# A hybrid decoder trunk in float32: four alternating seven-product units per down projection instead of five

## The reference

```python
def swiglu(h, w_gate, w_up, w_down):
    return (jax.nn.silu(h @ w_gate) * (h @ w_up)) @ w_down

x = x + 0.5 * swiglu(rms_norm(x, norm_w[l, 0]), ffn_w_gate[l, 0], ffn_w_up[l, 0], ffn_w_down[l, 0])
x = x + mixer(rms_norm(x, norm_w[l, 1]))
x = x + 0.5 * swiglu(rms_norm(x, norm_w[l, 2]), ffn_w_gate[l, 1], ffn_w_up[l, 1], ffn_w_down[l, 1])
```

## Time and profile before

| | us |
|---|---|
| median of 3 runs | 1131.41 (1130.73 to 1131.84) |
| the profiled execution | 1132.68 |
| its span in the trace | 1130.9 |
| PE busy | 1072.1 (95% of the span) |
| PE weight loads busy | 970.0 (86%) |
| DVE busy | 792.9 (70%) |
| ACT busy | 551.8 (49%) |

### The profile page before, as it was taken

The page is one execution under the profiler, slowest core; times in us unless marked ns, Lnnn a source line. Parts: engine busy times, 40 slices in busy tenths (PEclk is TensorE's granted clock), DMA queues, the critical chain, the costliest instruction groups (busy, mean ns, idle before and its releaser), DMA issues.

```text
span 1130.9 us, 19136 instructions
## 1 busy us (share of the span) xinstructions
PE 1072.1 (95%) x8333; PEld 970.0 (86%) x8333; DVE 792.9 (70%) x1011; ACT 551.8 (49%) x661; POOL 49.2 (4%) x32
## 2 busy tenths in 40 slices
PE   7999988999888999998989999898999999999978
PEld 7999966898777799997779999776788889999957
DVE  5877678698853587676768767676764647667676
ACT  5644345585672354443535444353754536444242
POOL 1000000110171000000000000000100000000000
PEclk9999999999898999999999999999999999999999
DMA  9855436363004275553457565356546465655341
GB/s 312 265 184 188 159 118 203 118 192 112 2 4 152 75 224 186 187 187 107 159 181 224 184 189 187 99 165 220 167 151 218 152 223 167 195 175 196 125 150 38
DMA packets 127197, 184.90 MB, mean 164 GB/s; under 512 B 4205, under 2 KB 101722, under 8 KB 126986
## 3 DMA queue, kind: packets, MB, share of 16 engines
q1 hardware_dynamic: 126368, 181.85, 49.6%
q0 software_dynamic: 448, 1.71, 0.5%
q10 hardware_dynamic: 298, 0.12, 0.0%
HBM read 182.62 MB, written 1.05 MB: 162 GB/s over the span
## 4 chain that ended last, share of the span: by engine, by line
PE 73%; DVE 17%; ACT 5%; issue 3%; DMA 1%; POOLq 0%; SPq 0%; POOL 0%; DVEq 0%; ACTq 0%
PE banks L1441 20%; PE banks L1442 20%; PE banks L1443 20%; DVE wlo L918 8%; ACT whi L482 4%; DVE rounded L996 2%; DVE arena L989 2%; PE banks L1877 2%; DVE raw L991 1%; DVE arena L990 1%; PE banks L1520 1%; PE banks L1524 1%; PE banks L1521 1%; PE banks L1603 1%; PE banks L1604 1%
## 5 line engine op out<-in xcount | busy, mean ns | idle before, releaser
L918 DVE TENSOR_TENSOR wlo<-raw,whi 128x2048 fp32r<-128x2048 f32 (+1 forms) x167 | 381.9, 2298 | 151.2 <-ACT whi L482 150.9
L482 ACT ACTIVATE whi<-raw 128x2048 fp32r<-128x2048 f32 (+1 forms) x171 | 322.9, 1904 | 253.0 <-PE banks L1443 136.5
L1441 PE MATMUL banks<-xTh,whi 128*128 128x256 f32 x1408 | 397.2, 282 | 0.8 <-DVE wlo L918 0.5
L1442 PE MATMUL banks<-xTl,whi 128*128 128x256 f32 x1408 | 396.2, 281 | 0.0
L1443 PE MATMUL banks<-xTh,wlo 128*128 128x256 f32 x1408 | 396.1, 281 | 0.0
L1441 PEld LDWEIGHTS banks<-xTh,whi 128*128 128x128 f32 x1408 | 265.9, 189 | 1.8 <-DVE wlo L918 1.0
L1442 PEld LDWEIGHTS banks<-xTl,whi 128*128 128x128 f32 x1408 | 266.1, 189 | 0.0
L1443 PEld LDWEIGHTS banks<-xTh,wlo 128*128 128x128 f32 x1408 | 266.0, 189 | 0.0
L1441 PE MATMUL banks<-whi,hTh 128*128 128x512 f32 (+1 forms) x180 | 78.5, 436 | 24.4 <-issue 24.3
L1442 PE MATMUL banks<-wlo,hTh 128*128 128x512 f32 (+1 forms) x180 | 74.8, 416 | 0.0
L1443 PE MATMUL banks<-whi,hTl 128*128 128x512 f32 (+1 forms) x180 | 74.5, 414 | 0.0
(11 more groups left out here) (277 smaller groups left out, 1403.1 us busy)
## 6 DMA issues: line engine op xcount, KB each, us to landing
raw<-in_ffn_w_up SPq DMA_DIRECT2D x44, 1024.0 KB, 5.4
raw<-in_ffn_w_down SPq DMA_DIRECT2D x44, 1024.0 KB, 4.9
raw<-in_ffn_w_gate SPq DMA_DIRECT2D x43, 1024.0 KB, 5.4
raw<-in_sg_w_in SPq DMA_DIRECT2D x16, 1024.0 KB, 5.6
raw<-in_ab_w_in SPq DMA_DIRECT2D x8, 1024.0 KB, 5.4
raw<-in_sg_w_out SPq DMA_DIRECT2D x8, 1024.0 KB, 5.3
raw<-in_ab_w_out SPq DMA_DIRECT2D x4, 1024.0 KB, 4.9
raw<-in_ab_w_in SPq DMA_DIRECT2D x2, 832.0 KB, 4.4
```

The source lines that it names most:

```text
L482: A(whi[:, j % SLOTS, 0:kt * width], raw[:, j % SLOTS, 0:kt * width], ACT.Copy).then_inc(S("hi_ready"), 1)
L918: TT(wlo[:, j % SLOTS, 0:n], raw[:, j % SLOTS, 0:n], whi[:, j % SLOTS, 0:n].bitcast(f32), ALU.subtract).then_inc(S("lo_ready"), 1)
L1441: mm(out_ap, lh, rh, start=first, stop=False)
L1442: mm(out_ap, lh, rl, start=False, stop=False)
```

## The change

The seven-product units are 2, 4, 6 and 8, each followed by a direct one. Of such a unit the three plain blocks (1536 columns) are rounded and split apart from the summed block, which goes with T_SUM. The orders on ACT and DVE are written out anew, the third and fourth down units (base + 24, base + 25) are now rounded and split inside the last gate/up pair, and the splits of the next stage's first two units stand among the x_updates. The load behind a seven-product unit waits for the lo of its summed block. The two buffers of T_SUM and T_HI change places.

```diff
-SEVEN = (2, 3, 5, 6, 8)
+SEVEN = (2, 4, 6, 8)
...
-        T_AT = [XT0 + 3072, XT0 + 1536]
-        T_SUM, T_HI, T_LO = [at(o, 1536) for o in T_AT], [at_r(o, 1536) for o in (R0 + 4096, XT0)], [at_r(o, 1536) for o in T_AT]
+        T_AT = [XT0 + 1536, XT0 + 3072]
+        T_SUM, T_HI, T_LO = [at(o, 1536) for o in T_AT], [at_r(o, 1536) for o in (XT0, R0 + 4096)], [at_r(o, 1536) for o in T_AT]
...
         def lo_done(j):
...
-            return S("lo_ready"), j + 1 - sum(1 for i in POOL_LO if i < j)
+            if j in SEVEN_UNITS:
+                n = SEVEN_UNITS.index(j)
+                return S("sums_lo"), 2 * N7 * (n // N7) + N7 + n % N7 + 1
+            return S("lo_ready"), j + 1 - sum(1 for i in POOL_LO + SEVEN_UNITS if i < j)
...
+        SEVEN_UNITS = [u_ffn[f] + 22 + i for f in range(4) for i in SEVEN]
...
             def hi(j):
...
-                A(whi[:, j % SLOTS, 0:kt * width], raw[:, j % SLOTS, 0:kt * width], ACT.Copy
-                  ).then_inc(S("hi_ready"), 1)
+                n = 1536 if j in SEVEN_UNITS else kt * width
+                A(whi[:, j % SLOTS, 0:n], raw[:, j % SLOTS, 0:n], ACT.Copy).then_inc(S("hi_ready"), 1)
...
+            def right_hi(f, k):
+
+                j = u_ffn[f] + 22 + SEVEN[k]
+                act.wait_ge(S("summed"), 2 * N7 * f + N7 + k + 1)
+                A(T_HI[k % 2], T_SUM[k % 2], ACT.Copy).then_inc(S("sums_hi"), 1)
+                A(whi[:, j % SLOTS, 1536:2048], raw[:, j % SLOTS, 1536:2048], ACT.Copy).then_inc(S("sums_hi"), 1)
...
                 for c in range(PAIRS_F):
-                    if c < PAIRS_F - 1:
-                        hi(base + 2 * c + 4)
+                    hi(base + 2 * c + 4)
                     silu_gate(f, c)
-                    if c < PAIRS_F - 1:
-                        hi(base + 2 * c + 5)
+                    hi(base + 2 * c + 5)
                     prod_hi(f, c)
...
+                d = base + 22
+                right_hi(f, 0)
+                hi(d + 4)
+                hi(d + 5)
+                right_hi(f, 1)
+                hi(d + 6)
+                hi(d + 7)
+                right_hi(f, 2)
+                hi(d + 8)
+                hi(d + 9)
+                right_hi(f, 3)
+                hi(d + 10)
+                hi(d + 11)
+                act.wait_ge(S("seven_sums"), 4 * f + 1)
+                A(V1, B[0][:], ACT.Copy).then_inc(S("p1_out"), 1)
+                hi(d + 12)
...
+            def base_lo(j):
+
+                dve.wait_ge(S("hi_ready"), j + 1)
+                TT(wlo[:, j % SLOTS, 0:1536], raw[:, j % SLOTS, 0:1536], whi[:, j % SLOTS, 0:1536].bitcast(f32),
+                   ALU.subtract)
...
             def right_lo(f, k):
...
+                dve.wait_ge(S("sums_hi"), 3 * N7 * f + N7 + 2 * k + 1)
+                TT(T_LO[k % 2], T_SUM[k % 2], T_HI[k % 2].bitcast(f32), ALU.subtract)
+                dve.wait_ge(S("sums_hi"), 3 * N7 * f + N7 + 2 * k + 2)
+                TT(wlo[:, j % SLOTS, 1536:2048], raw[:, j % SLOTS, 1536:2048], whi[:, j % SLOTS, 1536:2048].bitcast(f32),
+                   ALU.subtract).then_inc(S("sums_lo"), 1)
...
-            def next_x(s, factor):
-
-                for q in range(3):
-                    x_update(s - 1, q, factor)
+            def next_x(s, factor, j=None):
+
+                x_update(s - 1, 0, factor)
+                if j is not None:
+                    lo(j)
+                x_update(s - 1, 1, factor)
+                x_update(s - 1, 2, factor)
                 for k in range(4):
                     x_lo(s, k, s)
                 x_update(s - 1, 3, factor)
+                if j is not None:
+                    lo(j + 1)
                 for k in range(4, 8):
                     x_lo(s, k, s)
...
                     if c < PAIRS_F - 1:
                         lo(base + 2 * c + 4)
+                    else:
+                        base_lo(base + 24)
                     scale_up(f, c)
                     product(f, c)
-                    if c < PAIRS_F - 1:
-                        lo(base + 2 * c + 5)
+                    lo(base + 2 * c + 5)
                     prod_lo(f, c)
...
+                d = base + 22
+                right_sums(f, 0)
+                right_lo(f, 0)
+                base_lo(d + 4)
+                right_sums(f, 1)
+                lo(d + 5)
+                right_lo(f, 1)
+                base_lo(d + 6)
+                right_sums(f, 2)
+                lo(d + 7)
+                right_lo(f, 2)
+                base_lo(d + 8)
+                right_sums(f, 3)
+                lo(d + 9)
+                right_lo(f, 3)
+                lo(d + 10)
                 seven_added(f)
-                lo(base + 34)
                 factor = [0.5, 0.5]
                 if f < 3:
-                    next_x(s + 1, factor)
+                    next_x(s + 1, factor, d + 11)
...
                 begin(j)
-                pe.wait_ge(S("sums_lo"), 2 * N7 * f + N7 + k + 1)
                 pe.wait_ge(S("prod_lo"), PAIRS_F * f + i + 1)
```

More of the change, by code:

```diff
@@ L534, in prod_hi, with left_hi @@
                   ).then_inc(S("prod_hi"), 1)
-            def sums_hi(f, k):
+            def left_hi(f, k):
                 act.wait_ge(S("summed"), 2 * N7 * f + k + 1)
                 A(S_HI[k], S_SUM[k], ACT.Copy).then_inc(S("sums_hi"), 1)
+            def right_hi(f, k):
[3 more added lines that the diff above has]
+                A(whi[:, j % SLOTS, 1536:2048], raw[:, j % SLOTS, 1536:2048], ACT.Copy).then_inc(S("sums_hi"), 1)
             def ffn(f):
@@ L552, in ffn @@
                 for c in range(PAIRS_F):
-                    if c < PAIRS_F - 1:
-                        hi(base + 2 * c + 4)
+                    hi(base + 2 * c + 4)
                     silu_gate(f, c)
-                    if c < PAIRS_F - 1:
-                        hi(base + 2 * c + 5)
+                    hi(base + 2 * c + 5)
                     prod_hi(f, c)
                     if c in SEVEN:
[L560 to L571, removed]
+                        left_hi(f, SEVEN.index(c))
+                d = base + 22
[14 more added lines that the diff above has]
+                hi(d + 12)
                 if f < 3:
@@ L976, in left_lo @@
             def left_lo(f, k):
-                dve.wait_ge(S("sums_hi"), 2 * N7 * f + k + 1)
+                dve.wait_ge(S("sums_hi"), 3 * N7 * f + k + 1)
                 TT(S_LO[k], S_SUM[k], S_HI[k].bitcast(f32), ALU.subtract
@@ L993, in right_lo @@
             def right_lo(f, k):
-                dve.wait_ge(S("sums_hi"), 2 * N7 * f + N7 + k + 1)
-                TT(T_LO[k % 2], T_SUM[k % 2], T_HI[k % 2].bitcast(f32), ALU.subtract).then_inc(S("sums_lo"), 1)
+                j = u_ffn[f] + 22 + SEVEN[k]
+                dve.wait_ge(S("sums_hi"), 3 * N7 * f + N7 + 2 * k + 1)
[3 more added lines that the diff above has]
+                   ALU.subtract).then_inc(S("sums_lo"), 1)
             def seven_added(f):
@@ L1080, in ffn @@
                         left_sums(c, SEVEN.index(c))
-                for i in range(2, 11):
-                    if i in SEVEN:
-                        right_sums(f, SEVEN.index(i))
-                        lo(base + 22 + i)
-                        right_lo(f, SEVEN.index(i))
-                    else:
-                        lo(base + 22 + i)
-                lo(base + 33)
+                d = base + 22
[14 more added lines that the diff above has]
+                lo(d + 10)
                 seven_added(f)
-                lo(base + 34)
                 factor = [0.5, 0.5]
                 if f < 3:
-                    next_x(s + 1, factor)
+                    next_x(s + 1, factor, d + 11)
                 else:
```

## The result

The changed kernel takes 1084.83 us, the median of four executions (1082.72 to 1087.92), beside 1131.07 us for the kernel before on the same occasion; the ratio is 0.9611 (95% interval 0.9553 to 0.9670). It is 3.9% faster. The forecast was 1091.0 with a range of 1088 to 1098: the direction and most of the size were right, but the time lies 3 us under the range.

What follows compares the result with a forecast made beforehand. TensorE (PE) was taken as the bound, with stalls in the down stages. Stage gains of 9.5, 11.8, 11.8 and 7.3 us, together 40.4, took the median from 1131.41 to 1091.0 us, range 1088 to 1098.

Steps and rivals of the forecast that it cites:

- Part (a): Down stages on PE: four seven-product units instead of five add three matmuls a stage, costing 0.70 us each stage, 2.8 in all.
- Part (b): Between a down stage's last quarters: the transposes stay and cost 1.35 us.
- Part (c): New DVE and ACT order: a unit pair takes DVE 8.9 us against PE's 10.5, so the eight stalls go.
- no difference: Rival: the split order doesn't decouple DVE from ACT's rounding, DVE needing 10.9 us a pair; 1% chance.
- Part (d): Before unit 2 of each down stage: one new wait, 0.56 us a stage, bounds nothing to 1.5 us.
- Part (e): Stage end: splits moved behind x_updates remove PE's waits of 1.97 us and, in stages two and three, 3.8; margin 1.9.
- Part (f): DVE's work for the fifth unit's sums goes, off the path: nothing; slow clock stretches behind long waits go too.
- All that is edited acts inside these: The four down-stage spans of 70.27, 72.51, 72.52 and 66.46 us were taken to hold every effect of the edit.
- The clock did not fall behind the short wait before unit 2: Rival: each new wait before unit 2 brings 1.5 us of slow matmuls, 1097 us in all; 10% chance.
- The waits at the end did not stay: Rival: x_update(0) comes as late as before, three stages keep 2.0, 3.8 and 3.8 us: 1104, half 1097; 6%.
- DVE did not stay the bound: Rival: DVE's pair takes a sixth longer, needing PE's 10.5 us; some tenths lost, within the forecast; no chance given.
- loads landed in time: Rival of late loads, two at a time: beyond 10.5 us of landing PE waits; at 16 us, 1135 us; 2% chance.

Runs made afterwards that it cites:

- experiments 3: Kernel before with only the seven-product units set to 2, 4, 6, 8 and the buffers of T_SUM and T_HI changed round: 1100.36 us, ratio 0.9766.
- experiment 6: Kernel before with the alternation and the new stage-end order, plain and summed blocks still rounded and split together: 1083.64 us, ratio 0.9602.
- experiment 4: Kernel before with only the stage-end order changed, splits of the next stage's first two units moved among the x_updates: 1113.36 us, ratio 0.9879.
- experiment 11: Four weight loads held until the state loop's last step: kernel before 1124.29 us, changed kernel 1083.47, changed kernel with first sums ahead of unit 3's split 1080.91.
- experiment 2: The changed kernel run again with no edit: median 1083.48 us, ratio 0.9611.
- experiment 1: The kernel before run again with no edit, timed together with an unedited copy of the changed kernel: median 1125.46 us, ratio 0.9976.
- experiment 8: Extra 64-column matmuls early in the first FFN: four in the kernel before, 1124.30 us; 124 in the changed kernel, 1115.50 us.

## Why the prediction was wrong

**The terms.** Part (a), three matmuls a stage: PE has 8345 matmuls for 8333, as counted. Part (b), 1.35 us for the transposes: the stage with the first sums moved lasts 60.0, and 252 matmuls and 1.35 make 60.15. Part (c): no wait before units 4, 6 and 8. Its reason was right only in part: I gave the gain to the new order on DVE, with its idle 1.98 us filled; experiments 3 and 6 show that the alternation does it, with the old order inside a unit. With the old order a pair takes DVE 10.7 us (151.28 to 162.01 in experiment 6, the 1.98 us of idle time included) against PE's 10.5, so it is all but level, and the difference shows as the small delays of experiment 6. The rival of "no difference" had this number (10.9) and I drew nothing from it. Part (d): 0.58 us for 0.56. Part (e): right, by experiment 4 and the rows above. Part (f): the granted clock is 1.00 through all down stages in both profiles of the changed kernel.

**The step that failed** is the first sentence of the sum's frame: "All that is edited acts inside these", taken together with one profiled execution, 1132.68 us, as the base that the rest of the program would repeat. It was not a term of the stages: they were forecast to 40.4 us and gave 41.1 in the traces and 40.8 in experiment 11. The rest of the program was put at no change, and between the two profiles it gave 8.8 us more, 8.3 of them in the mixer of layer 0. The edit changed the number of PE's instructions ahead of the mixer, and with it the place where PE's stream is waited for in the state loop. In these two profiles 2.44 us in the open, ahead of a step that is on the path, became 0.72 us three matmuls earlier, and the slow stretch behind was gone: 5.8 of the 8.3 us. But the moved place is not enough: in experiment 2 the changed kernel had the slow stretch behind the moved wait too, and its mixer took 304.74 us.

**Chance** is the other part. With nothing edited, the executions of the kernel before lie between 1120.7 and 1134.5 in all its runs as baseline, and the baselines' medians between 1124.9 and 1131.1; three timings within 1.1 us of each other had looked like a narrow spread. The changed kernel lies at 1080.3 to 1089.3. Which waits the slow stretches follow differs from execution to execution, and the kernel before has eleven more long waits behind which they can fall. The base of the forecast, 1131.41, came from the upper end: the median of all 89 baseline executions is 1129.23, and with it the same 40.4 us lead to 1088.8; with the unedited copy's median (1125.46) they lead to 1085.1. The down stages of the kernel before vary as well: in the two profiles of experiment 1 the stages are 39.7 us apart, not 41.1. So how the 5.8 us between 46.2 and 40.4 divide between the moved wait and the draw of executions stays open.

**The rivals.** The clock did not fall behind the short wait before unit 2 in any profile. The forecast had leaned for this on one wait of 2.17 us without a fall, though six of the eleven waits had one. In the state loop PE idles for tenths of a us again and again, and the granted clock is 0.5 behind a wait of 1.5 to 2.5 us. The Trainium skill's rule ("TensorE: Matmul & The Clock Gate", section "A second HAM failure mode: psum-queue depth-cycling"), by which frequent short idles make the clock swing, would fit this loop better than the wait before unit 2. But the loop has the same short idles with the clock at 1.00 in all ten profiles without the long wait, so in the loop the traces put it down to the long one; the last section shows a fall without any wait. The waits at the end did not stay, DVE did not stay the bound, and loads landed in time.

**What stays open.** How much of the miss is the moved wait and how much the draw, as said above. Which of the mixer's waits the 4 us between 1082.7 and 1087 belong to in a given execution: that no execution is in the upper group once the loads are out of the loop speaks for the fetch, over 6 to 12 executions a kernel, not for all of it, as slow stretches that cost 1.1 to 1.6 us behind x_update's wait at the mixer's end remain. And it was not tried whether the fetch or the weight loads set the 0.7 us that remain.

## What to carry to other kernels

Before summing stage by stage, look at the stages that are not edited: a wait with no releaser beside full DMA engines may be the instruction fetch, and any edit of the instruction count ahead of it moves it, so it belongs in the range, to both sides. Slow stretches that come and go make one profiled execution a draw; several executions of the kernel before, not three close ones, tell how wide. And test an order's parts singly: here a change of four numbers and two moved lines did all that the long diff did.

## What the runs showed that I had not expected

**The fetch boundary.** Eight PE instructions more moved a wait of 2.44 us to one of 0.76, and 248 more in the other kernel brought 2.18 us back (experiment 8). This fits blocks of 256 instructions, and the traces have more for it than these two shifts. In the changed kernel's profile the waits of over 0.25 us in the loop that nothing releases stand 2286, 2032, 1905, 1778 and 1271 matmuls ahead of the second down stage: 127 apart, or a multiple of it (within one). With the weight loads 127 matmuls are 254 instructions.

**The pad.** Its 124 matmuls of 64 columns ran without a wait, and still the granted clock fell in the midst of them (stretches; then the first matmul behind the pad):

```profile
24.00:30.00 6.00, 6.00 (x54) 1.00 0.98 311
...
30.00:46.00 16.00, 16.00 (x77) 0.50 0.62 204
...
46.05 0.56 PE L1478 MATMUL banks<-xTh,whi 128*128 128x256 f32 x1
```

Up to the fall they come 0.112 us apart, close to the 0.12 us of a matmul of 256 columns in the same FFN; behind it they come 0.213 us apart, and the pad takes 21.5 us in all. The clock stayed low for 20.5 us, into the matmuls of 256 columns behind the pad. So a slow stretch does not need a wait ahead of it, and such a filler need not keep the clock up.
